# Two ways to form the remainder of an up-projection weight: VectorE's subtraction, or a transfer that adds

## The reference, cut to what matters

```python
def channel_mixer(h, w_up, ffn_dw_w, ffn_dw_b, w_down):
    u = causal_depthwise_conv(h @ w_up, ffn_dw_w, ffn_dw_b)
    a, b = jnp.split(u, 2, axis=-1)
    return (jax.nn.silu(a) * b) @ w_down
```

## Time and profile before

| | us |
|---|---|
| median of 3 runs | 2626.76 |
| lowest and highest run | 2626.3, 2628.7 |
| the profiled execution's own time | 2623.43 |
| span of the profiled execution | 2621.6 |
| TensorE busy in it | 2581.4 |
| VectorE busy in it | 1747.9 |
| ScalarE busy in it | 1086.5 |
| GpSimd busy in it | 67.9 |

### The profile page before, as it was taken

The page is one execution under the profiler, slowest core; times in us unless marked ns, Lnnn a source line. Parts: engine busy times, 40 slices in busy tenths (PEclk is TensorE's granted clock), DMA queues, the critical chain, the costliest instruction groups (busy, mean ns, idle before and its releaser), DMA issues.

```text
span 2621.6 us, 38515 instructions
## 1 busy us (share of the span) xinstructions
PE 2581.4 (98%) x15546; PEld 2229.8 (85%) x15546; DVE 1747.9 (67%) x2815; ACT 1086.5 (41%) x1685; POOL 67.9 (3%) x59
## 2 busy tenths in 40 slices
PE   8999999999999999999999999999999999999998
PEld 4789889877898899978888888888898888887997
DVE  5678777656787777757674458665677765387554
ACT  3546366535453675422223334222333222356442
POOL 0000000000000000100001010000000000100000
PEclk9999999999999999999999999999999999999999
DMA  8663467655634676464452213544435544231553
GB/s 329 229 194 111 148 208 248 220 196 196 198 108 172 221 244 217 151 215 178 161 193 91 98 62 137 185 153 145 145 122 193 187 170 163 82 121 65 179 184 113
DMA packets 120880, 441.13 MB, mean 168 GB/s; under 512 B 13312, under 2 KB 14720, under 8 KB 120192
## 3 DMA queue, kind: packets, MB, share of 16 engines
q1 hardware_dynamic: 120704, 438.68, 48.9%
HBM read 437.58 MB, written 1.05 MB: 167 GB/s over the span
## 4 chain that ended last, share of the span: by engine, by line
PE 93%; DVE 3%; ACT 2%; DMA 1%; issue 0%; SPq 0%; DVEq 0%; ACTq 0%
PE ps L657 24%; PE ps L658 24%; PE ps L659 24%; PE ps L661 14%; PE ps L654 5%; PE ps L655 3%; DMA ring<-stream 1%; DVE rests L1918 1%; PE ps L669 1%; ACT heads L1379 0%; DVE rs L1978 0%; DVE h_split L2034 0%; DVE rt L2025 0%; DVE rs L2018 0%; DVE rt L2182 0%
## 5 line engine op out<-in xcount | busy, mean ns | idle before, releaser
L657 PE MATMUL ps<-h_split,heads 128*128 128x256 f32 (+1 forms) x3192 | 1028.8, 322 | 7.1 <-DVE rests L1918 3.5
L658 PE MATMUL ps<-h_split,heads 128*128 128x256 f32 (+1 forms) x3192 | 1014.9, 318 | 0.0
L659 PE MATMUL ps<-h_split,rests 128*128 128x256 f32 (+1 forms) x3192 | 1014.6, 318 | 0.0
L1918 DVE TENSOR_TENSOR rests<-ring,heads 128x1024 fp32r<-128x1024 f32 x548 | 665.7, 1231 | 189.9 <-ACT heads L1379 182.9
L1379 ACT ACTIVATE heads<-ring 128x1024 fp32r<-128x1024 f32 x548 | 568.2, 1056 | 471.9 <-DMA ring<-stream 218.6
L657 PEld LDWEIGHTS ps<-h_split,heads 128*128 128x128 f32 x3192 | 610.0, 191 | 81.4 <-ACT rt L1558 15.1
L658 PEld LDWEIGHTS ps<-h_split,heads 128*128 128x128 f32 x3192 | 610.4, 191 | 42.3 <-issue 1.9
L659 PEld LDWEIGHTS ps<-h_split,rests 128*128 128x128 f32 x3192 | 610.1, 191 | 40.2
L1945 DVE SCALAR_TENSOR_TENSOR qt<-ring,silu_rows 128x1024 f32<-128x1024 f32 x240 | 286.5, 1231 | 5.2 <-issue 1.8
L657 PE MATMUL ps<-hid_split,heads 128*128 128x512 f32 (+1 forms) x660 | 236.3, 358 | 0.0
L659 PE MATMUL ps<-hid_split,rests 128*128 128x512 f32 (+1 forms) x660 | 235.7, 357 | 0.0
(11 more groups left out here) (229 smaller groups left out, 2425.2 us busy)
## 6 DMA issues: line engine op xcount, KB each, us to landing
ring<-stream SPq DMA_DIRECT2D x822, 512.0 KB, 3.5
consts<-constants SPq DMA_DIRECT2D x1, 1728.0 KB, 10.9
x_sb<-x_in SPq DMA_DIRECT2D x1, 1024.0 KB, 11.4
x_sb<-ctx_in SPq DMA_DIRECT2D x1, 1024.0 KB, 4.8
silu_rows<-rows_in SPq DMA_DIRECT2D x1, 1024.0 KB, 7.7
out<-area SPq DMA_DIRECT2D x1, 1024.0 KB, 4.8
consts<-constants SPq DMA_DIRECT2D x1, 704.0 KB, 9.3
cols<-columns SPq DMA_DIRECT2D x1, 538.5 KB, 10.1
```

What stands on the lines that cost most here:

```text
L657: nc.tensor.matmul(out, lhsT[0], rhs[0], start=first, stop=False)
L658: nc.tensor.matmul(out, lhsT[0], rhs[1], start=False, stop=False)
L659: ins = nc.tensor.matmul(out, lhsT[1], rhs[0], start=False, stop=last)
L1918: nc.vector.tensor_tensor(rests[:, u % RING, :], ring[:, u % RING, :], as_f32(heads[:, n % HEADS_RING, :]), ALU.subtract)\
```

## The change

In the up-projections of the first block, every split unit with an odd number (44 units, 22 in each layer) gets its rest in another way. ScalarE, behind the copy to `heads`, waits for that copy and writes minus the head into the ring slot, over the weights. GpSimd waits for that and issues a transfer that reads the unit from HBM a second time and adds it to what is in the slot, so that unit minus head stands there. TensorE waits for the head and for that transfer. VectorE leaves these units out. GpSimd's waits and transfers of a layer stand behind the sums of the norm ahead of the layer's up-projection.

```diff
--- before.py
+++ after.py
@@ -133,6 +133,11 @@
 def is_own(name):
 
     return name is not None and name.endswith(":own")
+
+
+def is_added(name, u):
+
+    return name is not None and name.startswith("up_") and u % 2 == 1
 
 
 def is_split(name):
@@ -518,6 +523,7 @@
         context_landed = sem("context_landed")
         rows_landed = sem("rows_landed")
         weights_landed = [sem(f"weights_landed{s}") for s in range(RING)]
+        rests_added = [sem(f"rests_added{s}") for s in range(RING)]
         output_stored = sem("output_stored")
 
         def col(name, k=0, n=1):
@@ -543,6 +549,9 @@
 
         def first_name(u):
             return (blocks[u * UB] or (None,))[0]
+
+        added = [u for u in split_units if is_added(first_name(u), u)]
+        added_so_far = {u: sum(a % RING == u % RING for a in added[:i + 1]) for i, u in enumerate(added)}
 
         own_left = [u for u in range(units) if is_own(first_name(u))]
 
@@ -636,7 +645,10 @@
                 u = b // UB
                 slot, at = u % RING, b % UB
                 split = is_split(name)
-                if at == 0 and split:
+                if at == 0 and u in added_so_far:
+                    pe.wait_ge(scalar_done, A.at(("heads", split_index[u])))
+                    pe.wait_ge(rests_added[slot], 16 * added_so_far[u])
+                elif at == 0 and split:
                     pe.wait_ge(vector_done, V.at(("rest", split_index[u])))
                 elif at == 0:
                     pe.wait_ge(weights_landed[slot], 16 * (u // RING + 1))
@@ -1320,12 +1332,21 @@
                       .then_inc(pool_done, G.mark((p, "sum") if k == SUMMED - 1 else None))
                     pool.wait_ge(pool_done, G.n)
 
+            def add_weights(name):
+
+                for u in added:
+                    if first_name(u) == name:
+                        pool.wait_ge(scalar_done, A.at(("minus heads", split_index[u])))
+                        pool.dma_start(rests[:, u % RING, :], stream[u, :, :], accum_op=ALU.add)\
+                          .then_inc(rests_added[u % RING], 16)
+
             in_block = lambda k: squared(SEQ, k)
             both_halves = lambda k: squared(TOK, k)
             for l in range(DEPTH):
                 if l > 0:
                     sums(("b1", l, "mix"), in_block)
                 sums(("b1", l, "ffn"), in_block)
+                add_weights(f"up_{l}")
             for v in (1, 0):
                 sums(("b2", 0, "f1", v), lambda k: squared_half(k, v))
             for l in range(DEPTH):
@@ -1378,6 +1399,10 @@
                     act.wait_ge(tensor_done, T.at(("unit", split_units[n - HEADS_RING])))
                 nc.scalar.activation(heads[:, n % HEADS_RING, :], ring[:, u % RING, :], ACT.Copy)\
                   .then_inc(scalar_done, A.mark(("heads", n)))
+                if u in added_so_far:
+                    own()
+                    nc.scalar.activation(rests[:, u % RING, :], as_f32(heads[:, n % HEADS_RING, :]), ACT.Copy, scale=-1.0)\
+                      .then_inc(scalar_done, A.mark(("minus heads", n)))
 
             def norm(p, T_, halves, updated, shift, rows_first=None):
 
@@ -1914,6 +1939,8 @@
                 u = split_units[n]
                 while own_left and own_left[0] < u:
                     mod_partial(own_left.pop(0))
+                if u in added_so_far:
+                    return
                 dve.wait_ge(scalar_done, A.at(("heads", n)))
                 nc.vector.tensor_tensor(rests[:, u % RING, :], ring[:, u % RING, :],
                                         as_f32(heads[:, n % HEADS_RING, :]), ALU.subtract)\
```

## The result

The changed kernel takes **2736.94 us** (median of 4 runs, 2725.49 to 2738.46) against 2626.53 us before, run beside it: ratio 1.0411, 95% interval [1.0396, 1.0427], 110 us slower. The forecast was 2677. The profiled execution is the lowest of the four, 2725.49 us, 102.06 above the profiled one of before; the rows add up to that figure.

The account below looks back on a forecast made before the run. TensorE, busy 98% of the span, was taken as the bound. A lag of 7.0 us closing a loop over two pairs cost 35 us in layer 0 plus 15 in layer 1: +50 on 2626.76, 2677 us; range 2639 to 2729.

Parts of the forecast that it names:

- lag 7.0: From negative copy's end until TensorE sees the added transfer: waking, issue, crossing and adding, taken as 7.0 us between 3.6 and 9.6.
- VectorE's freed time is worth nothing, ScalarE's copies too: Freeing 53.9 us of VectorE buys next to nothing; ScalarE's 44 negative copies, 1.09 us each with wait, cost nothing.
- The loop over two pairs: From one taking to that two pairs later: 9.59 + lag in layer 0, 7.62 + lag in layer 1, against 13.12 us.
- The parts 3.55 and 6.04: In layer 0's loop: taking to negative copy's end (1.40 + 1.06 + 1.09), and first matmul to taking, 6.04 us.
- the signs of being wrong: Wrong if TensorE's busy time grows, layer 1 loses as much as layer 0, or ScalarE, not DMA, ends TensorE's waits.
- Wake and issue, 0.14 + 1.1: Start of the lag: GpSimd wakes 0.14 us after ScalarE's result and takes 1.1 us to issue the transfer.
- The rival's GpSimd held by VectorE: Argument for the slow rival (15%): GpSimd's preparing of transfers could be held while VectorE works, 1.22 us at a time.
- Adding, 1.6: Part of the lag: reading the old contents costs as much as a second load, 1.6 us.
- The clock as a rival of its own: Rival: TensorE's clock falls after stalls, once in each of 10 loops, adding 17 us, 2694; with layer 1 2711; chance 15%.
- Slow: Rival: a lag of 9.6 us costs 61 us in layer 0 and 41 in layer 1, +102 us, 2729; chance 15%.

## Why the prediction was wrong

Turn by turn it closes. Two pairs of layer 0 took 13.12 us; the turn shown takes 504.39 - 483.95 = 20.44. Of the 7.32 more, 3.47 are the forecast (lag 7.0), 2.43 the rest of the lag (9.43), and 1.42 the half clock (7.46 - 6.04).

- *VectorE's freed time is worth nothing, ScalarE's copies too*: right, 0.9994 and 1.0009.
- *The loop over two pairs, 9.59 + lag in layer 0 and 7.62 + lag in layer 1*: right. The parts 3.55 and 6.04 are met to 0.02 us at full clock, half the transfers cost nearly as much, and moving the unit within its pair does what the formula says. Of the signs of being wrong, one came in part: TensorE's busy time in the two stages grew, by 14.6 and 14.9 us. The others did not: layer 1 lost less than layer 0, and ScalarE's head copies ended one wait of 3.7 us in layer 0, against 40.9 for DMA.
- *Wake and issue, 0.14 + 1.1*: right in the sum. GpSimd starts 0.36 us after the copy and issues in 0.86 to 1.02:

```profile
L1340 POOL DMA_DIRECT2D rests<-stream x44: 862/869/1016, 336.9 to 1102.1; - x44
...
DMA to landing us min/median/max: 5.3/7.2/9.4
```

The rival's GpSimd held by VectorE is not seen in these issues. The Trainium skill, SBUF — State Buffer, section Who interferes with whom, has two-input instructions of VectorE contend with GpSimd's reads only; the narrow spread of the issue time agrees.

- *Adding, 1.6*: right for the DMA engines (3.0 us in place of 1.5), small for the landing (7.2 in place of 5.1).
- *The lag, "I take 7.0, in between: the pairs will be stretched and the loads less crowded than now"*: **the step that failed.** Landing counts from the issue's start; the forecast's own figure for it was 5.8 to 7.7, 6.9 as taken, and the median of 7.2 is not far. But over the 20 waits of TensorE for a transfer, the time from the negative copy's end to the first matmul is 5.8 to 10.0 us, 8.4 in the median, and 9.1 to 9.7 in four waits of layer 0 that follow each other. First, the stretched pairs made no room: the DMA share rose from 0.76 and 0.74 to 0.80 and 0.88, and the loads' landing in layer 0 from 3.1/5.0/6.8 to 3.2/5.6/9.8. Second, a loop runs at the pace of its late transfers and not of the median one, and the late ones are those that meet loads. Of the 44, the 15 that found at most one of SP's loads on the way at the end of their issue landed in 6.3 us in the median; with 0.36 us until GpSimd issues and 0.14 from landing to first matmul that is a lag of 6.8, near the forecast's 7.0. The 20 that found three or more landed in 7.8, and the transfers of the four waits just named found three each. With 8.5 and 8.2, the medians of the waits in layer 0 and 1, the formula gives 20 x (9.59 + 8.5 - 13.12) / 2 = 50 and 20 x (7.62 + 8.2 - 13.12) / 2 = 27: 77 us, not 50. The Trainium skill's fit (DMA: Bandwidth & Descriptors, section Anatomy of one DMA — SWDGE (gpsimd) path), an estimated 4.9 us of lag, is further off; the plain transfer's least landing on GpSimd's queue, 3.5 us, is near its 3.2, the median of 5.1 is not.
- *The clock as a rival of its own, at 15%, with "a stall may fall into two of 1.7" against it*: the second failure. The stall is not shared out: it is 6.1 us in one pair of two. Rows showed after a gap of 0.7 us that the clock falls; a lag above the forecast only makes the gap longer, so Slow and Clock belonged together and not side by side. Not every stall cost clock: behind two of 3.1 and 3.3 us early in layer 0 the part from first matmul to taking stayed 6.02 and 6.03. What is left of the stages' 99.6 us after the 77 is 23, about 9 in layer 0 and 14 in layer 1. The turns with a wait bear that out: their part from first matmul to taking is longer than at full clock (6.04 and 3.15 us) by 9.9 in all in layer 0 and by 12.5 in layer 1. Layer 0's share was tested, with the scatter told above; layer 1's was not, and is read from such turns, here one with the longer part and one without:

```profile
1009.19 0.55 PE L669 MATMUL ps<-h_split,heads 128*128 128x256 f32 x1 [3.35 <-DMA rests<-stream]
1013.66 1.02 ACT L1583 ACTIVATE rt<-ps,cols 128x256 f32<-128x256 f32 x2 [4.96 <-PE ps L671]
...
1109.96 0.36 PE L669 MATMUL ps<-h_split,heads 128*128 128x256 f32 x1 [1.44 <-DMA rests<-stream]
1113.10 1.02 ACT L1583 ACTIVATE rt<-ps,cols 128x256 f32<-128x256 f32 x2 [2.44 <-PE ps L671]
```

The first has 4.47 us between the two, the second 3.14, the 3.12 of the formula.

The sum, in profiled executions: 50 forecast, 27 more lag, 23 clock, 100 of 102. That it closes so well is in part luck. The 13.12 us were read from 14 of the 20 pairs; over all 20, from the taking below to the last at 491.61, the kernel before took 126.75, or 12.68 for two, which adds 9 us to the forecast's sum. Against that, the first turn of each layer was shorter than the formula has it (12.2 us in layer 0, 12.9 in layer 1).

```profile
364.86 1.01 ACT L1558 ACTIVATE rt<-ps,cols 128x256 f32<-128x256 f32 x2
```

The median lies 11 us above the profiled run of the changed kernel; runs of kernels with this loop scatter more (13 us between lowest and highest, 4 before).

Still open is whether the loads on the way are what makes the late transfers late. SP issues its freed slots' loads in a bunch around the same time, six within 10 us of 481.07, and the engines are taken for 0.89 to 0.92 during the stall shown; that this delays the addition was read from those rows and from the landings above, not tried by itself. Making the heads of another pair ahead, which would hide the lag, was not tried either.

## What to carry to other kernels

Work taken off an engine that nobody waits for is worth nothing; ask instead what latency the new way puts between a buffer coming free and its next use, and close that loop with the latency of the late transfers in a crowded stage, not with the median. When the closed loop shows a stall, price the clock that falls in it in the same case. A transfer that adds should be counted as two on the DMA engines.

## What was not expected of the hardware

- An adding transfer of 512 KB holds the 16 DMA engines 3.0 us, a plain or rounding one 1.5 to 1.6; landing goes from 4.9 to 5.1 us to 7.2 to 7.8. GpSimd's issue of it takes 0.86 us against 0.53 for the plain one.
- An adding transfer that found three or more loads on the way landed in 7.8 us in the median, one that found at most one in 6.3.
- A plain transfer of GpSimd lands as soon as one from ScalarE's queue, 5.1 and 4.9 us, and the two kernels take the same time, 2679.33 and 2679.03 us.
- TensorE kept busy with useless products in a stall shortened the kernel by 17 us where they were shorter than the stall (4.5 us in 6.1), and lengthened it by 13 where they were longer (8.0).
